# Fewer and differently placed products around the layer norms of a hybrid decoder step

## What is computed

```
x  = layer_norm(ALPHA * x + mix, ln1_w, ln1_b)       # mix: gated linear attention and SSD (layer 0), HGRN2 (layer 1)
ff = moe(x)                                          # 16 experts in 4 groups, top 2
x  = layer_norm(ALPHA * x + ff, ln2_w, ln2_b)
layer_norm(x) = (x - mu) * rsqrt(mean((x - mu)**2) + EPS) * w + b
```

## Time and profile before

| | before |
|---|---|
| median of 3 runs, us | 944.75 (943.74 to 945.31) |
| the profiled execution, us | 943.86 |
| its span, us | 942.1 |
| PE / DVE / ACT / POOL busy | 96% / 40% / 30% / 11% |
| DMA queue of the weights (q1), share of 16 engines | 70.5% |
| mean granted TensorE clock | 0.990 |

### The profile page before, as it was taken

How to read it: one execution, slowest core, us unless ns; L and a number is a source line. 1 busy time by engine, 2 the same in 40 slices (tenths; PEclk the granted TensorE clock), 3 DMA queues, 4 the chain that set the end, 5 groups by cost and what they waited for, 6 DMA issues and landing times.

```text
span 942.1 us, 15920 instructions
## 1 busy us (share of the span) xinstructions
PE 901.3 (96%) x6591; PEld 564.1 (60%) x6591; DVE 372.5 (40%) x963; ACT 279.0 (30%) x595; POOL 103.3 (11%) x166
## 2 busy tenths in 40 slices
PE   8999999998999999999988798999999999999986
PEld 6878777675888344444425686777786343434424
DVE  2368776965314311111313225666327120201314
ACT  3534534232104120101003138788405120101003
POOL 2232130644000000000000000111400000000000
PEclk9999999999999999999999799999999999999998
DMA  9963354993997899999994963545798999999991
GB/s 376 349 251 141 110 195 155 351 386 144 419 422 290 299 421 418 421 421 421 420 418 201 413 257 140 182 142 178 265 418 337 393 421 419 420 420 421 421 398 57
DMA packets 41309, 299.86 MB, mean 318 GB/s; under 512 B 5064, under 2 KB 6600, under 8 KB 12808
## 3 DMA queue, kind: packets, MB, share of 16 engines
q1 hardware_dynamic: 36000, 268.52, 70.5%
q0 software_dynamic: 4544, 29.65, 8.5%
q10 hardware_dynamic: 688, 0.60, 0.2%
HBM read 283.32 MB, written 15.53 MB: 317 GB/s over the span
## 4 chain that ended last, share of the span: by engine, by line
PE 82%; DMA 9%; DVE 5%; issue 2%; ACT 1%; POOL 0%; SPq 0%; DVEq 0%; POOLq 0%; ACTq 0%
PE bank L1339 19%; PE bank L962 12%; PE bank L1363 10%; PE bank L1533 8%; PE bank L1209 6%; DMA ring<-in_w_down 6%; PE bank L1520 5%; PE bank L1405 3%; PE bank L1318 3%; PE bank L1230 3%; PE bank L1377 1%; DMA spread<-xd_rows 1%; DVE ring L2250 1%; DMA ring<-in_w_ab 1%; PE bank L1021 1%
## 5 line engine op out<-in xcount | busy, mean ns | idle before, releaser
L1339 PE MATMUL bank<-ring,W 128*32 128x512 f32 x1280 | 201.8, 593 | 3.2 <-DMA A<-in_w_up 1.7
L962 PE MATMUL bank<-xT,ring 128*128 128x264 f32 x704 | 164.1, 389 | 1.5 <-DMA ring<-in_w_ab 1.4
L962 PEld LDWEIGHTS bank<-xT,ring 128*128 128x128 f32 x704 | 131.5, 190 | 31.7 <-issue 8.8
L1339 PE MATMUL bank<-A,W 128*32 128x512 f32 x624 | 140.1, 593 | 0.0
L1339 PEld LDWEIGHTS bank<-ring,W 128*32 128x32 f32 x1280 | 55.8, 110 | 101.8 <-issue 96.3
L1363 PE MATMUL bank<-ring,W 128*32 128x512 f32 x528 | 77.1, 593 | 2.7 <-DMA ring<-in_w_down 2.7
L2523 DVE TENSOR_TENSOR gkg<-gkg,bank 128x512 f32<-128x512 f32 x16 | 11.0, 687 | 171.6 <-PE bank L1339 171.6
L1533 PE MATMUL bank<-xT,ring 128*128 128x264 f32 x320 | 78.0, 392 | 0.0
L1533 PEld LDWEIGHTS bank<-xT,ring 128*128 128x128 f32 x320 | 58.4, 190 | 11.0 <-issue 1.6
L1363 PE MATMUL bank<-A,W 128*32 128x512 f32 x288 | 62.7, 593 | 0.0
L1339 PEld LDWEIGHTS bank<-A,W 128*32 128x32 f32 x624 | 36.8, 110 | 36.8 <-issue 36.6
(11 more groups left out here) (345 smaller groups left out, 1256.0 us busy)
## 6 DMA issues: line engine op xcount, KB each, us to landing
ring<-in_w_gate SPq DMA_DIRECT2D x40, 1024.0 KB, 16.1
ring<-in_w_up SPq DMA_DIRECT2D x39, 1024.0 KB, 18.3
ring<-in_w_down SPq DMA_DIRECT2D x33, 1024.0 KB, 19.9
ring<-in_w_ab SPq DMA_DIRECT2D x10, 2048.0 KB, 8.8
A<-in_w_up SPq DMA_DIRECT2D x20, 1024.0 KB, 19.4
A<-in_w_gate SPq DMA_DIRECT2D x18, 1024.0 KB, 18.5
ring<-in_w_c SPq DMA_DIRECT2D x8, 2048.0 KB, 10.3
A<-in_w_down SPq DMA_DIRECT2D x13, 1024.0 KB, 12.8
```

The costliest lines, as they stand in the source:

```text
L962: mm = pe.matmul(ab_bank(m)[:, 0:T], slot(AB_IN0 + m // 4, 8)[:, c, (m % 4) * P:(m % 4 + 1) * P], xT[:, c, :], start=(c == 0), stop=(c == ...
L1339: mm = pe.matmul(out[ROWS * g:ROWS * (g + 1), :], xg[:, c, E_G * b + g, :], w[g][:, c % 4, :], start=(c == 0), stop=(c == DC - 1))
```

## The change

Three edits, all in PE's program. (1) `norm_squares` for odd k makes eight products over all 264 columns instead of eight of 128 and eight of 136; it waits only for the three squares of the second block. Both copies (in `finish_experts` and in `over_experts`) shrink. (2) `keep_clock` and its two calls go, fourteen products in each layer. (3) In layer 0, behind the last squares and before `settle_over`, two products of 512 columns are made into bank 5, which nothing reads then.

```
-                    for b, part in enumerate(BLOCK_PARTS):
-                        for j, (c0, c1) in enumerate(SCATTER):
-                            pe.wait_ge(sem("norm_squares"), SQUARES * (k // 2) + DC + 3 * b + j + 1)
-                            for c in range(c0, c1):
-                                mm = pe.matmul(square_bank(k)[:, part], ones[:, :], lnsq[:, c, part],
-                                               start=(c == 0), stop=(c == DC - 1))
+                    for j, (c0, c1) in enumerate(SCATTER):
+                        pe.wait_ge(sem("norm_squares"), SQUARES * (k // 2) + DC + 3 + j + 1)
+                        for c in range(c0, c1):
+                            mm = pe.matmul(square_bank(k)[:, 0:T], ones[:, :], lnsq[:, c, :],
+                                           start=(c == 0), stop=(c == DC - 1))
...
-                def keep_clock(count):
-
-                    for i in range(count):
-                        pe.matmul(bank[0][:, 0:P], ident[:, :], causal[:, :], start=True, stop=True)
-
                 stage_wait(pe, 3 * layer + 3)
-                keep_clock(10)
-
                 pe.wait_ge(sem("moe_chosen"), layer + 1)
...
-                keep_clock(4)
...
                 with pe.If(flag < 1):
                     norm_squares(2 * layer + 1)
                     if layer == 0:
+                        for i in range(2):
+                            pe.matmul(bank[5][:, :], ones[:, :], xacc[:, 0:2, 0:NP], start=True, stop=True)
                         settle_over()
```

## The result

| | before | changed |
|---|---|---|
| median of 5 runs, us | 944.16 (943.16 to 945.31) | 939.29 (938.43 to 940.54) |
| the profiled execution, us | 943.86 | 938.43 |
| its span, us | 942.1 | 936.6 |

The ratio is 0.9947 with a 95% interval of 0.9933 to 0.9962: faster by half a per cent. The forecast was 939.7. Repeated in a later group the changed kernel had 938.95 us (ratio 0.9957, 0.9941 to 0.9973).

What follows compares the result with a forecast made beforehand. PE, busy 96% of the span, was taken as the bound. From the median 944.75 us, -7.7 between the layers, 0, 0, -0.2 for dropped products and +2.85 for one hole at half clock gave 939.7 us; range 935.5 to 944.8.

Steps and rivals of the forecast that it cites:

- What the wait is: Between the layers, PE's 4.70 us standstill is an instruction fetch; the jump lands ten instructions before a block's end.
- the count of 112 instructions: Net instructions removed ahead of the jump's target, leaving some 120 instead of ten before the block's end.
- Its price, 7.7 us: Between the layers, the projection's chunk 7 ends at 523.2 instead of 530.9: 4.7 us wait, 3.0 us half clock.
- Part 2: The two new 512-column products behind layer 0's last squares take 1.7 to 2.2 us and cost 0.
- Part 3: The squares made over all columns change each layer by -0.2 to +0.2 us, taken as 0.
- Part 4: Dropping products ahead of the experts' gather gains 0.2 us but leaves idle holes, 2.85 us where the clock falls.
- one hole of the two: The clock falls ahead of the gather in one layer only, adding 2.85 us to the forecast.
- wait gone and both holes: The wait between the layers disappears, but the clock falls ahead of both layers' gathers: 942.6 us, chance 0.16.
- A: Between the layers the 4.70 us wait stays: 944.5 us without a hole, 947.4 with one; chance 0.11.
- B: Between the layers the wait is only shortened, half of 4.7 us left, clock kept: 942.2 us; chance 0.06.
- C: Clock falls ahead of the gather in both layers, 2.85 us each; with the wait kept 950.2 us, chance 0.05.

Runs made afterwards that it cites:

- pad of 3: The kernel before with three never-run products added in layer 0's overflow body, moving only the jump's target 12 instructions; 936.57 us, ratio 0.9928.
- pad of 28: The changed kernel with 28 never-run products in layer 0's overflow body, the jump's target again some ten instructions ahead of a block's end; 946.69 us, ratio 1.0039.
- 20 products: The changed kernel with 20 never-run products in layer 0's overflow body, the jump's target some 40 instructions ahead of the block's end; 940.48 us, ratio 0.9971.

## Why the prediction was right

**What the wait is: right.** The prediction read it as a fetch at a block's end ten instructions behind the jump, from one packet of the instruction queue and three matmuls. The runs with pads of 3, 28 and 20 products show the place as the cause, with waits of 0, 4.17 and 0.61 us, and confirm the count of 112 instructions. The jump over the overflow body itself took 3.3 to 3.4 us in both layers of the changed kernel, and 3.3 to 4.0 us in all profiles.

```profile
L1440 PEldq COMPARE_BRANCH  x2: 3296/3352/3409, 516.1 to 925.5; - x2
```

That these 3.3 to 4.0 us are a fetch as well was the author's reading, which no run tests. The traces agree with it: in the kernel before a packet starts 1.0 us into the jump of layer 0, and the jump ends 2.6 us behind the packet's start.

**Its price, 7.7 us: right** to 0.1. The two parts stand less neatly than they were split (4.7 wait, 3.0 half clock): the place alone is worth 6.0, the products 1.7. The half clock was read as what the wait does. But in the kernel before it began at 520.4, only 0.15 us into the wait, and without the wait it began as well: it follows the idle 2.7 us ahead of chunk 0. The wait keeps the clock low longer, 10.2 us (520.4 to 530.7) against 3.4 (518.4 to 521.8, in the run with the pad of 3). The traces give the clock as a share of full speed, 1.00 and 0.50 here; no run shows the figures in GHz that the prediction and the expectations put beside it.

**Part 2, products at no cost: right.** 1.88 us, done before chunk 0 was ready. That they "would not save the clock" with the wait in place: right, the clock fell there as well, at 526.6 us in the run with the pad of 28, in the wait itself:

```profile
526.00:527.00 1.00, 0.00 (x0) 0.00 (x0) 0.00 (x0) 0.00 (x0) 0.29 (x1) 0.81 0.99 410
```

**Part 3, squares at 0: right** (3.77 against 3.80 us; 10.75 against 10.78).

**Part 4: right in the sum only by two errors that cancel.** The chance was wrong: the forecast counts one hole of the two at half clock. That was my estimate of one chance in two for each layer, from a gap of 3.18 us that had cost once; no run shows such a chance, and in these fronts it was ten of ten. The price was wrong the other way: I took 2.85 for each from the projection's corner, and it was 1.5 in six fronts and 2.9 in four. That full weights make a fall dear isn't shown: at the restart of the earlier trace rows, with weights of 32 columns, it cost 1.4 to 1.6 us in five profiles and 2.8 in two. One times 2.85 and two times 1.5 come to nearly the same; in the second profile of the changed kernel the two fronts cost 4.4. What came, wait gone and both holes, had a chance of 0.16 and a time of 942.6. So it is luck that the single value, made for one hole, came within 0.4 us of the median. Rivals A and B don't hold: no issue time is left behind the jump. The fall that C names came in both fronts (0.69 and 0.68 in the windows above) and by itself gives back two fifths of the gain; with the wait in place it made the kernel slower, by 3.7 us against the kernel before beside it (946.69 and 942.95) rather than the 5.5 worked out (950.2 and 944.75).

## What to carry to other kernels

Where PE stands in "issue" some instructions behind a taken jump, look for a packet of the instruction queue just ahead of the restart, and move the jump's target by unrun instructions before anything else is tuned: twelve of them were worth 6 us here, and any edit of the program ahead of the jump moves it unasked. So a change that alters the instruction count has to be compared with its places held equal, or its parts are credited with what the layout did. Products that nothing reads are worth their place where PE would idle and dense work follows, if they end before that work can start. Here the stretches were 2.2 to 3.2 us long: ten products kept 1.5 to 2.9 us in each front, and two kept 1.3 to 1.7.

Of this change the place and the two new products made the gain; dropping the products in front of the experts cost some of it, 2.3 us in the medians of the one group that has both, 3.0 and 4.4 in the traces of the two profiles. The version with all of them (935.83 and 936.65 us) beats the kernel before, and the changed one by the traces. So does the kernel before with nothing but its target moved and the two products added (935.84): the rest of the change isn't needed.

## What the runs showed beyond that

With a gap of 3.2 us with only two products of 32 columns in it the clock fell in ten of ten fronts; with one of 2.0 us in one of two; with one of 2.2 to 2.7 us behind the squares in three of three. The length of a gap does not decide alone: at the restart of the earlier trace rows the clock stayed at 1.00 behind 3.48 us idle (first run with the fourteen put back) and fell behind 2.37 (changed kernel, 0.56 in 224 to 226 us). What decides it no run shows. The time at half clock behind such a gap was not the same from execution to execution of one program (gathers of 5.45 and 6.77 us in layer 0 of the two profiles of the changed kernel), 1.3 us where its times in the first result run from 938.43 to 940.54.

The wait is long where the second packet behind the jump comes late. Between the layers that packet started 6.1 to 6.9 us behind the first in all fourteen profiles, with a DMA share of 1.03 ahead of it; in the kernel before that is 3.9 us after the jump has ended. Behind layer 1's jump, with a DMA share of 0.03 to 0.04 in the kernel before, it started 3.0 to 3.7 us behind the first. That the weights' transfers make the difference is argued from these two places; no run took them away.
